# The four dependent steps of a head's solved values, half a tick later in the mixer rounds

## What is computed

```python
lower = jnp.where(tri_strict, jnp.einsum('bhncd,bhnsd->bhncs', k_beta, k) * decay, 0.0)
rhs = jnp.concatenate([v * beta[..., None], k_beta * jnp.exp(g)[..., None]], axis=-1)
sol = lax.linalg.triangular_solve(lower, rhs, left_side=True, lower=True, unit_diagonal=True)
...
v_new = ui - jnp.einsum('bhck,bhkv->bhcv', wi, state)
o = jnp.einsum('bhck,bhkv->bhcv', qd, state) + jnp.einsum('bhcs,bhsv->bhcv', qki, v_new)
```

## Time and profile before

| | us |
|---|---|
| median of 3 timed runs | 1208.64 |
| lowest and highest | 1208.52, 1208.86 |
| the profiled execution, its own time | 1204.78 |
| its span, first to last instruction | 1203.0 |
| TensorE busy in the span | 1170.6 (97%) |
| VectorE, ScalarE, GpSimd busy | 841.6, 701.7, 320.0 |

### The profile page before, as it was taken

The page is one execution under the profiler, slowest core; times in us unless marked ns, Lnnn a source line. Parts: engine busy times, 40 slices in busy tenths (PEclk is TensorE's granted clock), DMA queues, the critical chain, the costliest instruction groups (busy, mean ns, idle before and its releaser), DMA issues.

```text
span 1203.0 us, 21393 instructions
## 1 busy us (share of the span) xinstructions
PE 1170.6 (97%) x8616; PEld 1087.1 (90%) x8616; DVE 841.6 (70%) x1519; ACT 701.7 (58%) x1181; POOL 320.0 (27%) x257
## 2 busy tenths in 40 slices
PE   8999999999999999999999999999999999999997
PEld 7777899998877799998889999998989989999886
DVE  6796588884675579885568787888954565555456
ACT  5475576663458566664366667766667445444344
POOL 1172200000016300000166666575555320000000
PEclk9999999999999999999999999999999999999999
DMA  7633355556553356555343332332222646555542
GB/s 285 252 140 140 123 211 206 184 181 219 175 191 125 129 208 219 196 208 210 128 160 126 121 115 105 133 114 98 94 83 106 227 170 224 210 183 203 202 155 81
DMA packets 31587, 199.74 MB, mean 166 GB/s; under 512 B 4289, under 2 KB 6481, under 8 KB 8706
## 3 DMA queue, kind: packets, MB, share of 16 engines
q1 hardware_dynamic: 29506, 189.27, 43.6%
q0 software_dynamic: 1840, 8.60, 1.9%
q10 hardware_dynamic: 144, 0.52, 0.1%
HBM read 197.33 MB, written 1.05 MB: 165 GB/s over the span
## 4 chain that ended last, share of the span: by engine, by line
PE 83%; DVE 8%; ACT 4%; issue 2%; POOL 1%; DMA 0%; SPq 0%; POOLq 0%; DVEq 0%; ACTq 0%
PE ps L1182 24%; PE ps L1183 23%; PE ps L1184 23%; PE ps L1559 1%; PE ps L1575 1%; DVE ps L2824 1%; DVE wlo L2370 1%; PE ps L1336 1%; DVE conv L2755 1%; PE ps L1355 1%; PE ps L1323 1%; PE ps L1189 1%; PE ps L1207 1%; DVE halves L2472 1%; PE ps L1276 1%
## 5 line engine op out<-in xcount | busy, mean ns | idle before, releaser
L1182 PE MATMUL ps<-halves,whi 128*128 128x256 f32 x1472 | 409.8, 278 | 0.2
L1184 PE MATMUL ps<-halves,wlo 128*128 128x256 f32 x1472 | 404.8, 275 | 0.0
L1183 PE MATMUL ps<-halves,whi 128*128 128x256 f32 x1472 | 404.8, 275 | 0.0
L2370 DVE TENSOR_TENSOR wlo<-raw,whi 128x2048 fp32r<-128x2048 f32 (+1 forms) x133 | 301.3, 2268 | 112.2 <-ACT whi L1839 108.7
L1839 ACT ACTIVATE whi<-raw 128x2048 fp32r<-128x2048 f32 (+1 forms) x143 | 269.5, 1887 | 102.4 <-PE ps L1184 96.3
L1182 PEld LDWEIGHTS ps<-halves,whi 128*128 128x128 f32 x1472 | 282.5, 192 | 0.8 <-DVE halves L2963 0.5
L1184 PEld LDWEIGHTS ps<-halves,wlo 128*128 128x128 f32 x1472 | 282.6, 192 | 0.0
L1183 PEld LDWEIGHTS ps<-halves,whi 128*128 128x128 f32 x1472 | 282.5, 192 | 0.1
L1106 POOL TENSOR_TENSOR wlo<-raw,whi 128x1024 fp32r<-128x1024 f32 x72 | 172.5, 2404 | 51.0 <-ACT whi L1848 50.4
L1000 POOL TENSOR_TENSOR rstd<-sumsq,half_power 128x1 f32<-128x1 f32 x14 | 11.3, 809 | 573.3 <-ACT xn L1866 406.0
L1182 PE MATMUL ps<-whi,halves 128*128 128x512 f32 (+4 forms) x440 | 148.2, 337 | 4.8 <-DVE halves L2472 4.0
(11 more groups left out here) (337 smaller groups left out, 1849.5 us busy)
## 6 DMA issues: line engine op xcount, KB each, us to landing
raw<-in_stream SPq DMA_DIRECT2D x176, 1024.0 KB, 4.8
gain<-in_gains POOLq DMA_DIRECT2D x7, 512.0 KB, 5.7
bias<-in_rel POOLq DMA_DIRECT2D x1, 1536.0 KB, 8.6
raw<-in_stream SPq DMA_DIRECT2D x2, 648.0 KB, 7.3
cst<-in_consts POOLq DMA_DIRECT2D x1, 1280.5 KB, 5.9
raw<-in_stream SPq DMA_DIRECT2D x2, 528.0 KB, 4.2
x<-in_x SPq DMA_DIRECT2D x2, 512.0 KB, 4.3
out<-xn SPq DMA_DIRECT2D x4, 256.0 KB, 2.5
```

Source lines behind the costliest of these rows:

```text
L1182: nc.tensor.matmul(out, a_hi, b_hi, start=start, stop=False)
L1183: nc.tensor.matmul(out, a_hi, b_lo, start=False, stop=False)
L1184: return nc.tensor.matmul(out, a_lo, b_hi, start=False, stop=stop)
L2370: dve.tensor_tensor(used(wlo, n), used(raw, n), used(whi, n).bitcast(F32), ALU.subtract)\
```

## The change

The contents of the chain's two functions on TensorE change places: crossed and the products of o are now in `chain_first`, in ticks 1 and 2, and first and second solved in `chain_second`, in ticks 0 and 1. So each of the four steps comes half a tick later. ScalarE's two scalings move from ticks 0 and 1 to 1 and 2, and its `chain` call to the start of the tick, ahead of `level`, the evacuation and the split of the weights. VectorE's `rest` stays in tick 1 and moves behind the first part of the long taps.

```diff
# TensorE, chain_first (now crossed and the products of o)
+                if i == 1:
+                    pe.wait_ge(*S["first_values"].at((h, 1)))
+                    for r in range(2):
+                        last = nc.tensor.matmul(ps[:, 6, (1 - r) * P:(2 - r) * P], cross[:, h % 2, r, :],
+                                                values[:, first_tile(r), :], start=True, stop=True)
+                    last.then_inc(*S["crossed"].one(h))
+                if i == 2:
+                    pe.wait_ge(*S["second_values"].at((h, 1)))
+                    for t in range(TT):
...
+                    last.then_inc(*S["o_product"].one(h))
+
+            def chain_second(h, i):
+
+                if not 0 <= h < HEADS:
+                    return
                 if i == 0:
                     pe.wait_ge(*S["solution_sum"].at(h))
                     if h:
...
                     last.then_inc(*S["second_solved"].one(h))
-
-            def chain_second(h, i):
-
-                if not 0 <= h < HEADS:
-                    return
-                if i == 0:
-                    pe.wait_ge(*S["first_values"].at((h, 1)))
...
-                    last.then_inc(*S["crossed"].one(h))
-                if i == 1:
-                    pe.wait_ge(*S["second_values"].at((h, 1)))
...
-                    last.then_inc(*S["o_product"].one(h))
# ScalarE, chain
-                if i == 0:
+                if i == 1:
                     act.wait_ge(*S["first_solved"].at(h))
...
-                if i == 1:
+                if i == 2:
                     act.wait_ge(*S["second_solved"].at(h))
# ScalarE, the loop
+                    chain(r - 2, i)
                     level(r - 1, i)
                     if finished_slot(r, i):
                         evacuate(finished_slot(r, i))
...
-                    chain(r - 2, i)
                     level_late(r - 1, i)
# VectorE, the loop
-                    chain(r - 2, i)
                     level_first(r - 1, i)
...
                     long_taps(r * TICKS + i, 0)
+                    chain(r - 2, i)
                     level_second(r - 1, i)
```

More of the change, by code:

```diff
@@ L1622, in chain_first @@
                     return
+                if i == 1:
[7 more added lines that the diff above has]
+                    for t in range(TT):
+                        out = ps[:, 6, TOK + t * P:TOK + (t + 1) * P]
+                        r = 1 - t
+                        nc.tensor.matmul(out, qk_cross[:, h % 2, r, :], values[:, first_tile(r), :], start=True, stop=False)
+                        nc.tensor.matmul(out, qk_ratio[:, h % 2, t, :], values[:, t, :], start=False, stop=False)
+                        last = nc.tensor.matmul(out, qk_ratio[:, h % 2, 2 + t, :], values[:, 2 + t, :], start=False, stop=True)
+                    last.then_inc(*S["o_product"].one(h))
+            def chain_second(h, i):
+                if not 0 <= h < HEADS:
+                    return
                 if i == 0:
@@ L1636, in chain_first @@
                     last.then_inc(*S["second_solved"].one(h))
-            def chain_second(h, i):
-                if not 0 <= h < HEADS:
-                    return
-                if i == 0:
-                    pe.wait_ge(*S["first_values"].at((h, 1)))
-                    for r in range(2):
-                        last = nc.tensor.matmul(ps[:, 6, (1 - r) * P:(2 - r) * P], cross[:, h % 2, r, :],
-                                                values[:, first_tile(r), :], start=True, stop=True)
-                    last.then_inc(*S["crossed"].one(h))
-                if i == 1:
-                    pe.wait_ge(*S["second_values"].at((h, 1)))
[L1650 to L1655, removed]
-                    last.then_inc(*S["o_product"].one(h))
             def conv_norm(i):
```

## The result

The changed kernel takes 1209.54 us (median of 22 runs, 1206.61 to 1211.72), the kernel before, run beside it, 1206.70 us (22 runs, 1204.21 to 1211.23). The ratio of all runs together is 1.0018, 95% interval 1.0012 to 1.0025: the change costs about 2.2 us, between 1.4 and 3.0 (the two medians by themselves differ by 2.8). The forecast was +0.7 us.

A forecast was written before the change was run, and what follows sets the result against it. TensorE, busy 1170.6 of 1203.0 us, bounds the kernel, so the change acts only through its gaps. Terms 0 (rounds 2 to 5) - 0.1 (6, 7) + 0.4 (8) + 0.4 (9) = +0.7, on 1208.64: 1209.3 us, range 1207.4 to 1211.4.

The forecast's parts named there:

- no change of over 0.2%: Whole kernel: time within about 0.2% (2.4 us) of the kernel before, chance 0.83.
- Rounds 2 to 5, "nothing, 0 us": Rounds 2 to 5: the moved steps' inputs arrive in time and VectorE's wait covers the later evacuation; 0 us.
- The sign of being wrong: New waits for `prod` in rounds 2 to 5, or step 2 later there, would speak for B.
- B: Rival: ScalarE's values ahead of the qk evacuation delay VectorE, then TensorE in rounds 2 to 7; +3.6 beside +0.7, chance 0.11.
- Rounds 6 and 7, the chain: Rounds 6 and 7: waits for `solved` and `rest` give way to waits for `inv_t` and `prod`; -0.1 us together.
- The wait for `inv_t`: Sign in the new profile: TensorE's wait for `inv_t` grows from 1.4 to about 3.5 us over rounds 6 to 8.
- Round 8, +0.4: Round 8: first solved loses cover; later products of o delay the squares and `conv_rsd`; +0.4 us, bounds 0 and +1.1.
- Round 9, +0.4: Round 9: first solved comes after the waits for the rounded convolution, losing 0.44 us of cover; +0.4 us.
- A: Rival: the addressed TensorE waits vanish and nothing takes their place; -4.3 us, 1204.3, chance 0.04.
- C: Rival: no change, the 0.44 us of rounds 8 and 9 also covered; 1208.6, chance 0.22.
- D: Rival: partial gain, rounds 6 to 8 keep half of their 4.3 us; -2 us, 1206.7, chance 0.05.

The follow-up runs named there:

- experiment 1: Changed kernel, GpSimd's low half ahead of the deviation of o in tick 2 of rounds 2 to 7: 1207.90 us, ratio 1.0005 to the kernel before.
- experiment 2: Kernel before, one added GpSimd `pow` between deviation of o and low half, tick 2 of rounds 2 to 7: 1223.30 us, ratio 1.0134.
- experiment 3: Kernel before, two tiny GpSimd instructions delaying the low half in tick 2 of rounds 2 to 7: 1210.37 us, ratio 1.0012.
- experiment 4: Kernel before, one tiny GpSimd instruction delaying the low half in tick 2 of rounds 2 to 7: 1208.01 us, one run only.
- 5: Changed kernel, VectorE's qk gate of rounds 2 to 7 moved behind tick 3's first long taps and final o: 1206.42 us, ratio 0.9995.
- experiment 7: Changed kernel, first solved of heads 6 and 7 (rounds 8 and 9) back in the middle of tick 0: 1208.20 us, ratio 1.0008.
- experiment 10: Changed kernel, low half first (rounds 2 to 7), `conv_rsd` first (round 8), first solved of heads 6 and 7 back in tick 0: 1205.94 us, ratio 0.9983.
- 9: Kernel before, GpSimd's low half (rounds 2 to 7) and `conv_rsd` (round 8) ahead of the deviation of o in tick 2: 1207.19 us, ratio 0.9993.
- experiment 6: Changed kernel, ScalarE's `chain` call behind `level` and the evacuation instead of ahead of them: 1210.52 us, ratio 1.0024.

## Why the prediction was right or wrong

The time fell in the range, and no change of over 0.2% was the likeliest class. The size was a third of the true one: +0.7 against +2.2. That 1209.3 stands beside a measured 1209.54 is luck. The forecast was added to 1208.64, the median of three runs, and the 22 runs beside the change put the kernel before at 1206.70; the base too high by 1.9 us more than made up for the 1.5 us that were missing.

**Rounds 2 to 5, "nothing, 0 us": the step that failed** (+1.05 us in the table), with the odd round 7 beside it (+0.43 for -0.05). Its figures were met one by one (719.89 for 719.97, 721.56 for 721.6, step 3's join without its wait). But it followed only what waits for the four moved steps by a semaphore on TensorE, VectorE and ScalarE. For round 8 I followed the products of o further, through the squares to GpSimd. In rounds 2 to 7 I didn't, although the same deviation stands there ahead of a low half of 2.4 us, in the same tick. The row to read was GpSimd's L1106 at 725.06, ending as VectorE's gate begins. I took GpSimd's lateness as harmless, since TensorE needs its weights three ticks later. That was true for the weights and missed the neighbour. By experiment 1 the held gate costs 1.5 us over rounds 2 to 7, where the forecast had 0 and -0.1; experiments 2 to 4 bring the same pattern into the kernel before, and 5 shows the way to TensorE. The sign of being wrong did its work, new waits for `prod` in rounds 3 and 5, but it pointed at B.

Why odd rounds: in the even ones a second short convolution follows in VectorE's program. In round 4 VectorE's wait there shrinks from 0.68 us (first row, before) to 0.21 us (second row, after), which is the lateness taken up:

```profile
767.30 3.21 DVE L2755 SCALAR_TENSOR_TENSOR conv<-ps,par,conv 128x254 f32<-128x254 f32 x8 [0.68 <-ACT conv L2058]
```

```profile
770.71 3.21 DVE L2755 SCALAR_TENSOR_TENSOR conv<-ps,par,conv 128x254 f32<-128x254 f32 x8 [0.21 <-ACT conv L2058]
```

The forecast did look for such covers, but only for the lateness of the evacuation.

**Rounds 6 and 7, the chain:** right, but for the 0.1 us, of which experiment 1 shows nothing (both rounds at +0.01). In round 7, less 3.85 us (the offset of that round), the transposes come at 850.57 (forecast 850.52) and step 1 at 857.86 (forecast 857.85):

```profile
854.42 0.66 PE L1541 MATMUL ps<-ident,inv_t 128*128 128x128 f32 x4 [1.13 <-POOL inv_t L1098]
...
861.11 0.71 PE L1654 MATMUL ps<-rest,solved 128*128 128x128 f32 x4 [0.23 <-DVE rest L2901]
861.71 0.55 PE L1559 MATMUL ps<-prod,inv_t 128*128 128x128 f32 x3
```

The wait for `inv_t` was forecast at about 3.5 us in all and is 4.9. Its old 1.4 us, the 2.0 us of `solved` that it takes over and three times the lost 0.44 us make 4.7; the forecast had left the last part out of this sign.

**Round 8, +0.4:** measured +0.20. By the experiments it is the sum of three parts: +0.44 for first solved without cover (experiment 7), about -0.8 for the wait for `rest` (experiment 10 against 9), and +0.57 for `conv_rsd`. The last is the difference between what its removal gives in the changed kernel (1.42) and in the kernel before (0.85). Less that round's 4.28 us, step 1 came at 891.70 (forecast 891.9) and the squares at 895.69 (forecast 895.9): against the kernel before step 1 gained 0.48 us beside the 1.26 of o, where the forecast had 0.3. The mechanism was right, and the gain at `rest` 0.2 us too small.

**Round 9, +0.4:** measured +0.40, by the mechanism named.

**Rivals:** A (-4.3) falls as argued: `inv_t` took the place. B had the right place on TensorE, `prod` in the rounds 2 to 7, by the wrong cause, as experiment 6 shows. C falls, since the interval leaves out no change, and D, since nothing was gained.

## To carry to other kernels

When an instruction is moved, follow its whole tail, also through the engines with slack, until it meets something that stands beside another engine's work and not only before it. An engine off the critical path can take time from its neighbour with no semaphore between them: in the trace this is an instruction that starts on time and lasts longer. And add the gaps as chains with a second releaser: of the 4.3 us of waits here, the later chain had 0.8 us, and only after the tail was put right.

## What the runs showed of the hardware

**VectorE's gate and GpSimd's low half nearly exclude each other.** In every trace here in which a low half ended more than 0.15 us behind the start of the first gate instruction (all six of rounds 2 to 7 in the changed kernel and in experiments 2 to 4, rounds 3 to 7 in 5), that instruction ended 0.28 to 0.32 us behind the low half. The overlaps ran from 0.3 to 0.9 us, and the instruction takes 0.43 alone. So its price was the overlap less 0.11 to 0.15 us: 0.39 of overlap made it last 0.67 us, 0.61 made it 0.89, 0.67 made it 0.95. Had the two only slowed each other, the end of the one would not be tied to the end of the other like that. The low half gives way too: beginning within the second gate instruction it took 2.52 us in place of 2.38. This is that row, GpSimd's next low half after the gate, in the changed kernel:

```profile
731.32 2.52 POOL L1106 TENSOR_TENSOR wlo<-raw,whi 128x1024 fp32r<-128x1024 f32 x1 [0.38 <-ACT whi L1848]
```

The gate reads two tensors from SBUF (`tanh`, `conv`). The long taps, whose second tensor is in PSUM, show nothing of the kind: in the changed kernel 144 of them lie for over half their length beside a low half and take 0.47 to 0.51 us, the 58 wholly free ones 0.47 to 0.49. Nor do the short taps (L2755), also with one of their tensors in PSUM: 0.47 to 0.48 us beside a low half and free. The Trainium skill, page "SBUF — State Buffer", section "Who interferes with whom", states that a VectorE instruction with two SBUF inputs takes its second one through the read interface shared with GpSimd; it calls the shared ports an exclusive lock and says that the order of issue decides who blocks. The trace agrees in the main, with two differences. The gate loses its overlap less 0.11 to 0.15 us here, so its row doesn't grow by the whole overlap. And in round 2 of experiment 2 the low half's row begins 0.07 us ahead of the second gate instruction, yet it is the low half that grows (2.77 us) and the gate that doesn't (0.45 us), while in round 5 a lead of 0.05 us held the gate for 2.59 us; so the starts in the rows don't settle who gives way when they lie that close. That the two SBUF inputs are the reason was not isolated by a run of its own: the traces show that the gate is held and the taps aren't.

**The price is not proportional to the delay.** In round 3, against the round's begin, the low half starts 0.38, 0.60, 0.66 and 0.87 us later than before the change in experiment 4, the changed kernel, experiment 3 and experiment 2. Over rounds 2 to 7 that cost TensorE 0.7, 1.5, 1.8 and 13.5 us. The jump comes where the next low half begins just ahead of the second gate instruction and holds it to its own end, in five of the six rounds.
